# The handover from the experts to the second block in a float32 kernel: last tiles by column halves, norm factors applied to results

## What is computed

```python
h = h + mixed @ w_out
hn = rms_norm(h, ffn_norm_gain)
h = h + peer(hn, ...)                    # experts: sum over 16384 rows of expert_up, weighted
x = rms_norm(h, final_norm_gain)         # end of the first block

h = rmsnorm(x, norm_mix_g)               # second block
c_g, b_g, xa, za, q, fl, iv, og, ga, gb = jnp.split(h @ w_in, split_idx, axis=-1)
ya = b_g * causal_dwconv3(c_g * xa, conv_w) * jax.nn.silu(za)
# log_f, kk from fl;  o = hgrn2_chunked(silu(q), kk, iv, log_f), normed per head
yb = o * jax.nn.silu(og)
m = sigmoid(ga) * (ya @ w_a_out) + sigmoid(gb) * (yb @ w_b_out)
x = x + m @ w_o
gate = sigmoid(rmsnorm(x, ple_norm_g) @ w_ple_gate)
x = x + gate * (p @ w_ple_proj)
return rmsnorm(x, final_norm_g_2)
```

## Time and profile before

| | |
|---|---|
| median of three runs | 2857.69 us (2855.1 to 2858.04) |
| the profiled execution | 2856.41 us |
| its span, first to last instruction | 2854.6 us |
| PE busy | 2796.9 us (98%) |
| DVE busy | 1820.0 us (64%) |
| ACT busy | 1403.9 us (49%) |
| POOL (GpSimd) busy | 580.7 us (20%) |
| share of the chain that ended last: PE, DVE, ACT | 92%, 3%, 3% |
| mean granted TensorE clock | 0.994 |
| read from HBM | 535.31 MB |

### The profile page before, as it was taken

How to read it: one execution, slowest core, us unless ns; L and a number is a source line. 1 busy time by engine, 2 the same in 40 slices (tenths; PEclk the granted TensorE clock), 3 DMA queues, 4 the chain that set the end, 5 groups by cost and what they waited for, 6 DMA issues and landing times.

```text
span 2854.6 us, 38995 instructions
## 1 busy us (share of the span) xinstructions
PE 2796.9 (98%) x14968; PEld 2405.3 (84%) x14968; DVE 1820.0 (64%) x2908; ACT 1403.9 (49%) x1984; POOL 580.7 (20%) x262
## 2 busy tenths in 40 slices
PE   8999999999999999999999999997999999999998
PEld 6888888888888888888888888886888889999886
DVE  5566766877777655555555555556677866555555
ACT  5444644455555544454444444445645545444454
POOL 0000000388888888600000000000000000000000
PEclk9999999999999999999999999998999999999999
DMA  7654478877777777767767777764564546666564
GB/s 254 210 160 120 140 239 320 238 190 189 190 191 189 190 188 190 195 213 224 222 208 223 220 231 234 221 210 136 173 188 149 163 152 186 185 190 187 183 194 153
DMA packets 199017, 559.00 MB, mean 196 GB/s; under 512 B 53472, under 2 KB 69872, under 8 KB 195888
## 3 DMA queue, kind: packets, MB, share of 16 engines
q1 hardware_dynamic: 161456, 554.99, 63.3%
q0 software_dynamic: 36944, 0.41, 2.8%
q10 hardware_dynamic: 432, 1.11, 0.1%
HBM read 535.31 MB, written 21.12 MB: 195 GB/s over the span
## 4 chain that ended last, share of the span: by engine, by line
PE 92%; DVE 3%; ACT 3%; issue 1%; DMA 0%; DVEq 0%; ACTq 0%
PE bank L506 92%; ACT whi L1499 1%; DVE wlo L856 1%; PE bank L518 1%; ACT scr L1499 0%; ACT QKb L1499 0%; DMA cols<-in_cols 0%; ACT L1499 0%; DVE tmpc L859 0%; DVE aX L897 0%; DVE QKb L859 0%; DVE X L1238 0%; ACT DD L1499 0%; ACT aX L1499 0%; ACT EB L1499 0%
## 5 line engine op out<-in xcount | busy, mean ns | idle before, releaser
L856 DVE TENSOR_TENSOR wlo<-raw,whi 128x1024 fp32r<-128x1024 f32 (+1 forms) x965 | 1179.6, 1224 | 871.0 <-ACT whi L1499 867.8
L1499 ACT ACTIVATE whi<-raw 128x1024 fp32r<-128x1024 f32 (+1 forms) x965 | 1017.3, 1056 | 1021.1 <-PE bank L506 1010.3
L506 PE MATMUL bank<-aX,whi 128*128 128x512 f32 (+1 forms) x4000 | 968.4, 392 | 0.0
L506 PE MATMUL bank<-whi,aX 128*128 128x512 f32 x3008 | 932.7, 390 | 13.2 <-ACT whi L1499 11.8
L506 PEld LDWEIGHTS bank<-aX,whi 128*128 128x128 f32 (+1 forms) x4000 | 729.6, 188 | 143.0 <-issue 3.0
L506 PEld LDWEIGHTS bank<-whi,aX 128*128 128x128 f32 x3008 | 565.7, 188 | 132.2 <-ACT whi L1499 11.8
L1481 POOL DMA_INDIRECT gate_scratch<-gate,place x256 | 577.9, 2257 | 263.0 <-DMA gate_scratch<-HB 184.7
L506 PE MATMUL bank<-wlo,aX 128*128 128x512 f32 x1504 | 586.6, 390 | 1.4 <-DVE wlo L856 1.4
L506 PE MATMUL bank<-aX,wlo 128*128 128x256 f32 (+1 forms) x3984 | 531.4, 284 | 4.5 <-DVE wlo L856 2.3
L506 PEld LDWEIGHTS bank<-aX,wlo 128*128 128x128 f32 (+1 forms) x3984 | 513.6, 191 | 26.0 <-DVE aX L897 3.0
L506 PEld LDWEIGHTS bank<-wlo,aX 128*128 128x128 f32 x1504 | 282.9, 188 | 61.6 <-DVE wlo L856 3.5
(11 more groups left out here) (212 smaller groups left out, 1669.9 us busy)
## 6 DMA issues: line engine op xcount, KB each, us to landing
raw<-in_w_down SPq DMA_DIRECT2D x256, 512.0 KB
raw<-in_w_up SPq DMA_DIRECT2D x256, 512.0 KB
raw<-in_w_in SPq DMA_DIRECT2D x176, 512.0 KB
raw<-in_w_out SPq DMA_DIRECT2D x32, 512.0 KB
gate_scratch<-HB SPq DMA_DIRECT2D x16, 1024.0 KB, 7.1
raw<-in_w_pq SPq DMA_DIRECT2D x32, 512.0 KB
raw<-in_w_o SPq DMA_DIRECT2D x32, 512.0 KB
raw<-in_w_pg SPq DMA_DIRECT2D x32, 512.0 KB
```

The costliest lines, as they stand in the source:

```text
L506: return e.matmul(o, lhsT, rhs, start=start, stop=stop, skip_group_check=True)
L856: e.tensor_tensor(wlo[:, s, 0:n], raw[:, r, 0:n], whi[:, s, 0:n].bitcast(F32), ALU.subtract).then_inc(s_lo, 1)
L1499: return e.activation(o, i, f, **k)
```

## The change

- The last eight expert tiles (120 to 127) run all their half-0 units first, then all their half-1 units. `NW` becomes 8.
- The bare residual sum (no norm factor, no gain) is turned: `end_turn` for kp 0 to 3 in the ticks of units UP1-7 to UP1-4, for kp 4 and 5 after UP1, for kp 6 and 7 after UP1+1. The turned tiles are split with the product of both gains (`C_NMX` x `C_FIN`). Tile kt lies in row (kt + 8) % 16 of `aX`.
- `fl` 0 to 3 run side by side: four first halves (kt 0 to 7), then four second halves.
- Squares, sums and roots of both norms are done in `finish(x)` beside the units around UP1; GpSimd multiplies the residual by `grow1` for the second norm's squares. The product of both factors goes to a diagonal, PE turns it to rows after unit UP1+11 (`rows4`).
- GpSimd multiplies every result of `fl`, `q2`, `og`, `cg`, `xa`, `bg`, `za`, `ga`, `gb` (128 x 256 each, 88 in all) by `rows4`; its readers wait for `s_rw`. `iv` is scaled as it is copied out.
- The `lbs` chain moves into the experts' loop (i 96 to 106). `decay` starts one unit later, the turns of `DD` two units later.
- `cols` is loaded ahead of the two first weight units.
- The last `pp` unit finishes token half 0 first. GpSimd multiplies columns 0 to 1535 by `grow2` earlier; the last products are shared by DVE and ACT.

```diff
+    def side_by_side(self, name, key, js, fills):
+        at = len(self.src)
+        for i, fill in enumerate(fills):
+            self.h += 1
+            self.groups[name, i] = Group([at + i, at + len(js) + i], [fill], self.h)
+        self.src += [self.I[key][j, u] for u in range(2) for j in js]
...
-    for i in range(128):
-        plan.src += [I["w_up"][i, u] for u in range(2)]
+    UPS = [(i, half) for i in range(120) for half in range(2)] + [(i, half) for half in range(2) for i in range(120, 128)]
+    plan.src += [I["w_up"][i, half] for i, half in UPS]
...
-            if 70 <= k < 74:
+            if 72 <= k < 76:
...
+            if UP1 - 7 <= u < UP1 - 3:
+                end_turn(u - UP1 + 7)
+            if u in (UP1, UP1 + 1):
+                for kp in (4, 5) if u == UP1 else (6, 7):
+                    end_turn(kp)
+            if u == UP1 + 11:
+                w.wait_ge(s_one2, 1)
+                row_of(R4F, 3, ones2, diag2)
...
+        def end_turn(kp):
+            for k in (kp // 2, 4 + kp // 2):
+                evacuated(UPF[k])
+            turn_two("mix", kp, X2)
...
         # DVE
+        def finish(x):
+            if x in (-7, -6, -1, 0):
+                w.wait_ge(s_mm, UP0 + 248 if x < -1 else UP1)
+                w.wait_ge(s_h1r, 128)
+                g = {-7: 0, -6: 1, -1: 2, 0: 3}[x]
+                for t in range(2):
+                    b, o = UPB[4 * t + g], X2[:, t, g * 512:g * 512 + 512]
+                    tt(o, banks[b], HB[:, t * D + g * 512:t * D + g * 512 + 512], ALU.add).then_inc(s_free[b], 1)
+            if -5 <= x < -1:
+                low_two("mix", x + 5)
+            if x in (1, 2):
+                low_two("mix", 2 * x + 2)
+                low_two("mix", 2 * x + 3)
...
-            evacuated(G["cg", i].fills[0])
-            evacuated(G["xa", i].fills[0])
+            w.wait_ge(s_rw, RESCALE["xa", i])
...
-            evacuated(G["bg", i].fills[0])
+            w.wait_ge(s_rw, RESCALE["bg", i])
...
-        for t, g, x in gained_rows("out", 48, X2, grow2):
-            x.then_inc(s_fin, 1)
+        w.wait_ge(s_gg, 6)
+        w.wait_ge(s_rinv, ROWS["out"])
+        for t, a in ((0, 1024), (1, 768)):
+            r = st[:, 24 + t:25 + t]
+            e.scalar_tensor_tensor(X2[:, t, 1536:D], X2[:, t, 1536:D], r, grow2[:, 1536:D], ALU.mult, ALU.mult).then_inc(s_fin, 1)
+            e.tensor_scalar(X2[:, t, a:1536], X2[:, t, a:1536], r, None, ALU.mult).then_inc(s_fin, 1)
...
         # GpSimd
+        for n in range(8):
+            g, t = n // 2, n % 2
+            f = slice(g * 512, g * 512 + 512)
+            w.wait_ge(s_nt, TURNED["mix", 2 * g + 1][1] + 1)
+            w.wait_ge(s_sqa, 17 + n)
+            e.tensor_tensor(X2[:, t, f], X2[:, t, f], grow1[:, f], ALU.mult).then_inc(s_z, 1)
+        w.wait_ge(s_free[R4F[0]], R4F[1])
+        for name, i in RESCALED:
...
+            w.wait_ge(s_free[b], n)
+            e.tensor_tensor(h, h, rows4[:, :], ALU.mult).then_inc(s_rw, 1)
+        w.wait_ge(s_row2, 16)
+        for i in range(3):
+            for t in range(2):
+                f = slice(i * 512, i * 512 + 512)
+                w.wait_ge(s_sqa, 40 + 2 * i + t + 1)
+                e.tensor_tensor(X2[:, t, f], X2[:, t, f], grow2[:, f], ALU.mult).then_inc(s_gg, 1)
...
         # ACT
+        def finish(x):
+            if -6 <= x < -2:
+                high_two("mix", x + 6)
+            if x in (1, 2):
+                high_two("mix", 2 * x + 2)
+                high_two("mix", 2 * x + 3)
...
+            if 4 <= x < 8:
+                g = x - 4
+                for t in range(2):
+                    w.wait_ge(s_z, 2 * g + t + 1)
+                    square(X2[:, t, g * 512:g * 512 + 512], scr[:, t, g * 512:g * 512 + 512], 8 + 4 * t + g)
+            if x in (8, 9):
+                root()
+            if 14 <= x < 18:
+                t, f = x % 2, slice((x - 14) // 2 * 1024, (x - 14) // 2 * 1024 + 1024)
+                w.wait_ge(s_rinv, ROWS["fin"])
+                act(X2[:, t, f], X2[:, t, f], ACT.Copy, scale=st[:, 24 + t:25 + t]).then_inc(s_x2, 1)
...
+        e.dma_start(cols[:, :], I["cols"]).then_inc(s_cols, 16)
         for u in range(2):
             e.dma_start(raw[:, u, :], plan.src[u]).then_inc(s_raw[u], 16)
-        e.dma_start(cols[:, :], I["cols"]).then_inc(s_cols, 16)
```

More of the change, by code:

```diff
@@ L74, with __init__ @@
 class Group:
-    def __init__(self, first, n, fills, halves):
-        self.first, self.end, self.fills, self.halves = first, first + n, fills, halves
-        self.units = range(first, first + n)
+    def __init__(self, units, fills, halves):
+        self.units, self.fills, self.halves = units, fills, halves
+        self.first, self.end = units[0], units[-1] + 1
 class Plan:
@@ L651, in tick, with unit_x, group_x @@
                 ple_turn(PLE_TURN[u])
-        def group_x(name, i, ready):
+        def unit_x(g, o, u, ready, row):
+            s, j = u % NSPL, g.units.index(u)
+            final = u == g.end - 1
+            for high in (False, True) if j else (True, False):
+                w.wait_ge(s_hi if high else s_lo, u + 1)
+                for k in range(8):
+                    kt = 8 * j + k
+                    ready(kt)
+                    if high:
+                        last = mm(o, whi[:, s, k * 128:k * 128 + 128], aX[:, row(kt), :], kt == 0, final and k == 7)
+                    else:
+                        last = mm(o[:, 256:512], wlo[:, s, k * 128:k * 128 + 128], aX[:, row(kt), 0:256], False, False)
+            last.then_inc(s_mm, 1)
+            tick(u)
+        def group_x(name, i, ready, row=lambda kt: kt):
             g = G[name, i]
@@ L656, in group_x @@
             for u in g.units:
[L657 to L669, removed]
+                unit_x(g, o, u, ready, row)
         def group_f(name, i, xh, xl, ready):
@@ L816, in _ @@
-        norm_turn("mix", 0, scr)
-        for name in ("fl", "q2"):
-            for i in range(8):
-                group_x(name, i, normed("mix"))
+            w.wait_ge(s_hi, u + 1)
+            w.wait_ge(s_lo, u + 1)
+            for t in range(2):
+                c = slice(t * 128, t * 128 + 128)
+                for g in range(2):
+                    k, f = t * 4 + half * 2 + g, slice(g * 512, g * 512 + 512)
+                    o = vacant(UPF[k]) if i == 0 else banks[UPB[k]]
+                    mm(o, wring[:, i % NW, c], whi[:, s, f], i == 0, False)
+                    mm(o, wring[:, i % NW, c], wlo[:, s, f], False, False)
+                    last = mm(o, wring[:, i % NW, 256 + t * 128:384 + t * 128], whi[:, s, f], False, i == 127)
@@ L1371, in _ @@
+        for j in range(2):
+            for i in range(4):
+                step(G["fl", i].units[j])
+                if j:
+                    whole(G["fl", i], kh[:, i, :])
+        for i in range(4, 8):
             g = G["fl", i]
@@ L1640, in step @@
                 root()
+            if UP1 - 6 <= u < UP1 + 18:
+                finish(u - UP1)
             if u in MIX_TURN:
@@ L1859, in _ @@
         root()
+        w.wait_ge(s_gg, 6)
+        w.wait_ge(s_rinv, ROWS["out"])
+        for t, z in ((0, 1024), (1, 768)):
+            act(X2[:, t, 0:z], X2[:, t, 0:z], ACT.Copy, scale=st[:, 24 + t:25 + t]).then_inc(s_fia, 1)
 def arrays(inp):
```

333 lines of the change are left out of this document (186 added, 147 removed).

## The result

The changed kernel takes 2840.39 us (median of five executions, 2838.87 to 2841.45), the kernel before 2857.69 us: a ratio of 0.9941 with a 95% interval from 0.9927 to 0.9956 (below, the interval stands in brackets behind each ratio). 17.3 us are won; 23.4 were forecast. The profiled execution has a span of 2837.3 us against 2854.6.

The account below looks back on a forecast made before the run. TensorE, busy 2796.9 of 2854.6 us, bounds the kernel, so only idle and slow-clock stretches can be won. Terms -20.0 - 3.5 - 2.4 - 1.5 + 4 = -23.4 us give a median of 2834, range 2826 to 2843.

Parts of the forecast that it names:

- Handover: From the last expert unit to the `fl` units: 24.7 us lost there, less transposes, row-factor matmuls and a stall, 20.0 won.
- One new stall: Near unit UP1-7, PE waits 0.95 us for the residual adds of column group 0, behind a split on DVE.
- Rival 3: Handover does not close: late root chain or POOL's 128x512 products make PE wait, 3 to 6 us, 2839; 0.24 with rival 1's mild form.
- GpSimd's price: Rescaling products on GpSimd make others wait: 2 us in the rounds, 1 for `og`, 1 in the last stage; 4 us lost.
- `cg` to `za`: Recurrence rounds: DVE and ACT wait for POOL products, 3.0 us asked of 3.1 idle per round; 2 us charged over six rounds.
- Rival 1: GpSimd and DVE hold each other up under the recurrence: 2847 (chance 0.08), milder 2840 (0.24 together with rival 3).
- The turns of `DD`: In the recurrence, transposes two units later remove PE's one 3.5 us wait for `DD`: 3.5 us won.
- What is late next is the last `og` tile: After moving the `DD` turns, the next late thing is needed by the cut four and more units on: costs nothing.
- The start: With `cols` loaded first ACT starts 4.3 us earlier, but bytes of the fifth weight tile bind: 2.4 us won, ends 0 and 4.3.
- The end: Last `pp` matmuls by token half let DVE start earlier, 1.35 us, and a shorter first output piece, 0.15: 1.5 us won.
- Rival 2: GpSimd becomes the pace in `cg` to `za`: products from 1.8 us eat all gains, at 2.26 us 2870; chance 0.03.
- Rival 4: All covers hold and the start goes by ACT alone: 4 us less price, 1.9 more start, 1 from decay, 2827; chance 0.12.

Follow-up runs that it names:

- experiment 5: Changed kernel with the expert weights of tiles 115 to 122 made one tile earlier, three tiles ahead instead of two: 2837.65 us, ratio 0.9933.
- experiment 3: Changed kernel with all 88 GpSimd products done on a tile nobody reads, nobody waiting, results left unscaled: 2833.47 us, ratio 0.9919.
- experiment 2: Changed kernel without the 32 GpSimd products of `cg`, `xa`, `bg`, `za`, those results left unscaled: 2832.27 us, ratio 0.9914.
- experiment 8: Kernel before with only unused bytes per partition added: 32 bytes 2854.73 us, 96 bytes 2850.80 us, 96 and 2560 bytes 2851.20 us.

## Why the prediction was right, and where it was not

The forecast was 2834.0 us with a range of 2826 to 2843; the kernel took 2840.39. It lies in the range and on the forecast's side, but partly by luck: an error of 5 us in favour, which has nothing to do with the change's mechanism, stood against larger ones the other way. Without it the kernel would take 2845 us, outside the range.

- **Handover, -20.0: measured -16.6.** The mechanism is as told: no wait for `ones2` or the diagonal, clock 1.00, PE's one wait for a residual add 1.1 us where 0.95 was said, turns that take some 0.4 us for four, as counted. The step that failed is "One new stall". There was a second one, the weights' look-ahead (1.2 us, experiment 5). The text followed the splits and adds through steps UP1-7 and on, but not `weight`, which is paced in tiles while the order is now in units. Another 1.0 us was never there to win: the 24.7 us were measured to ACT's pick-up of the last `fl` result, and in both kernels ACT, released by PE, first does a split and picks up 0.96 us later (2018.33 before, 1998.94 after). The last 1.2 us are spread over small losses that no row singles out. Rival 3 (it does not close, 3 to 6 us) is near this size, by another cause.
- **GpSimd's price, +4: measured +8.6 (stretches) to +9.8 (medians)** for the 88 products, and 0.8 more in the last stage, where 1 was taken (two PE waits of 0.3 us for `wlo` are new there; no run leaves out the six products alone). The term mis-sized is `cg` to `za`, 2 us forecast, 6.1 measured (8.1 by the medians). The single wait was sized well (0.78 said, 0.86 measured) and a product as well (0.68 against 0.75). What failed is "Just in, on average; with uneven steps I charge 2 us": 3.0 us asked of 3.1 us room, in a stage with bursts. Two small terms were wrong as well: `og`, 1 us forecast, cost nothing that shows, and `q2`, put at nothing, cost 2.2 us in units 700 to 715, by products that stretch `wlo` (experiment 3). Waiting is the larger part of the whole, 5.6 of 8.6 us (6.9 of 9.8 by the medians). Rival 1's mechanism is in the trace (1.65 and 1.76 us) but is worth 2.8 us; its mild form, 2840, is the number that came out, and that is no evidence for it. Against it the text held that DVE stands still in three of four cases; but 13 of the 88 products lasted over 1.3 us, six of them among the eight of `qh`. The sign of being wrong that the text had set, over 10 us of PE waits for `wlo` in the rounds, did not come: they were 6.5 us.
- **The turns of `DD`, -3.5: measured 0 in the stretch, -1.2 by the waits.** The failed step is "What is late next is the last `og` tile". Late next was DVE's own `wlo` behind the reduce and the scalings. The text moved the turns and said itself that DVE's work ahead of them is not moved. Of the new 3.5 us wait 2.3 are there without the rounds' products too (experiment 2), and 1.2 came with them. It also took the stall at its 3.5 us and no more; the clock behind it (0.57, 1.3 us) is in the kernel before, and after the change it falls again behind the new 3.5 us wait.
- **The start, -2.4: measured about -1.** ACT's first product came 5.4 us earlier (4.54 instead of 9.89 us) and only some 1 us of it was left at unit 40: bound by bytes as argued, not by ACT; the fifth tile landed at 22.1 us where 21.4 was worked out.
- **The end, -1.5: measured -1.55.** As told.
- **Where the change does nothing, 0: measured some -5.** 0.9 us in units 80 to 120 and 3.9 from 800 to 935, by the offset of 96 bytes (experiment 8); the rest of the line from 40 to 640 lies where executions scatter. The text listed what was counted at nothing, and tile addresses were not on the list. With this term known the same sum would have been 2829.

Rival 2 (GpSimd becomes the pace) falls: a product alone is 0.74 us where 1.8 were needed. Rival 4 falls with the start and the price.

## What to carry to other kernels

A wait names what came last, not what is late: before counting a wait as won, follow the engine that released it through its queue, and ask what stands there if the awaited thing moves. When the order of units changes, every helper that is paced by another count (here weights by tile) must be followed too. An operation that somebody waits for costs its wait each time, whatever the mean idle time says; three products of 0.43 us on the busy engine (2.1 us in all rounds) were cheaper than four on an idle one (6.1 us). And a change that allocates tiles can move the time of untouched stages: compare stretches with the same instructions first.

## What the runs showed of the hardware

- PE's pace changed with the addresses of the tiles that it reads: 0.234 or 0.229 us for a 512-column matmul of `wo`, by 96 bytes of padding; 5 us of 2857 in all.
- The same 3.5 us stall brought the granted clock down to 0.57 in one execution and left it at 1.00 in another, 1.3 us apart; behind stalls of 2.3 us it fell once (0.57) and stayed at 1.00 twice.
- GpSimd's product of 128x256 lasts 0.74 us with DVE idle and up to 1.7 us beside it, and stretched the DVE operation behind it from 1.22 to 1.76 us.
